# Small projections on 32-column strips, shared reciprocals, keys and values by transposes, and a gather in two halves, in a two-layer diffusion backbone

## The chip, the cores and the metric

The kernel runs on one core of one Trainium2 chip. The metric is the device time of one launch in microseconds (us), the median of several runs. Engines are named PE (TensorE; its weight loads are PEld), DVE (VectorE), ACT (ScalarE), POOL (GpSimd) and SP (SyncE, which issues the weight DMAs).

## The reference, cut to what matters

Two trunk layers work on 384 tokens (128 context, 256 latent) of width 1024, in fp32:

```
h = rms_norm(x, norm1_g) * (1 + sc1) + sh1            # sc, sh, g: silu(c) @ ada_w
proj = h @ w_in
A: q, k, v = silu(short_conv(proj[qa, ka, va]))       # 12 channels of 128, 5 taps
   q = l2_norm(q) * 128**-0.5;  k = l2_norm(k)        # 4 heads each
   beta = sigmoid(...);  g = -rate * softplus(...)    # 16 small columns of proj
   chunked gated delta scan, forward and backward
B: chunkwise mLSTM scan over qb, kb, vb               # and 16 small gate columns
C: windowed grouped-query attention over qc, kc, vc, rotary on the latents
mixed = sig(ga) * (ya @ wa) + sig(gb) * (yb @ wb) + sig(gc) * (yc @ wc)
x += g1 * (mixed @ w_out)
h = rms_norm(x, norm2_g) * (1 + sc2) + sh2
aff = softmax(h @ w_router);  gates, idx = top_k(aff.T, cap)     # 16 experts
xs = h[idx]                                            # 32 latent + 16 context rows each
ye = (silu(xs @ w_gate) * (xs @ w_up)) @ w_down * gates
x += g2 * scatter_add(ye, idx)
```

## The kernel before

The hidden state stands as hT, eight tiles of 128 features by 384 tokens. One Fori over the two layers holds everything. Each engine has its own program, written out in order by hand; what an engine produces is counted on a semaphore (a mark in a "track" such as conv_act or ring_used), and the consumer waits for that count. All weights come as 2 MB blocks (eight tiles of 128x512) that SP loads in order into a ring of four slots, six for the experts; per layer 32 blocks and then 48 of the experts (gate, up, down for each of 16). A slot is loaded again when PE has marked the block in it as used.

PE uses three forms of projection. `channels` (L757) has the weights stationary and 384 tokens moving, eight matmuls for 128 output features. `tokens` (L764) has 128 tokens of hT stationary and 256 or 512 weight columns moving, for output in token layout. `ada_block` (L805) puts 32 matmuls of 128 columns side by side on four strips of 32 partitions. Transposes are all at L729.

The stages of a layer, in PE's order, with the lines that matter here:

- norm and modulation; then the small projection of the 32 gate columns (L825: 24 matmuls with hT stationary, 32 columns moving).
- twelve conv channels (L757). Behind each, ACT copies the bank to a padded tile (copies are all at L1514), DVE does five taps (L1922, L1924), ACT does silu. For the eight q and k heads ACT squares (L1602), PE sums the squares over the 128 partitions with a matrix of ones (L845), ACT takes the root (L1611), and DVE a reciprocal (L1931) and a multiply (L1933), each on 128x384. The gates' chain (DVE, ACT, and prefix sums on PE, L853 and L856) stands ahead of the fourth channel.
- delta rule: decay rows (L874), k-k products (L880), token-layout transposes, four ada blocks (L805), then the inverses and the scan.
- mLSTM: queries and keys by channels, transposes of the delta rule's output, the keys once more in token layout (L764, 128x256), a selection product (L1076), q-k product (L1089), values (L764, 128x512).
- attention: q and k by channels, k and v in token layout (L764, 128x256), rotary (L1244).
- merge of the branches, output projection, second norm.
- router: L1382 (24 matmuls, 16 columns moving), softmax and top-k on DVE, the selection matrices sel (L2308) and, weighted, selG (L2310), transposes of selG, and the gather (L1429, L1431), in which hidden rows in token layout are stationary and sel moves; DVE copies out (L2317, L2318), and POOL copies one expert's columns to a tile of its own (L717) and clears a tile (L710).
- experts, a Fori of two turns of eight: gate and up (L1460), silu, product on DVE (L2336), transposes, down (L1485), copies, and a combine (L1443, L2327) that scatters four experts at a time back to xT.

```
def squared_length(j):
    pe.wait_ge(done["conv_act"], at("conv_act", l, ("sq", j)))
    ...
    mm(PS[:, 4 + j % 4, 0:N], ones, sq_in[:, j % 2, :], start=True, stop=True)...
```

## Time and profile before

| | us |
|---|---|
| median of 3 runs | 2071.69 (2068.59 to 2072.93) |
| profiled execution, its own time | 2070.92 |
| its span | 2069.2 |
| PE busy | 1771.0 (86%) |
| DVE busy | 666.7 (32%) |
| ACT busy | 496.2 (24%) |
| POOL busy | 154.3 (7%) |
| moved by DMA | 344.63 MB, 167 GB/s over the span |

Times in the trace count from the span's start. Most fp32 matmuls leave two records, so x16 in a row of the timeline is eight matmuls; transposes leave one. A row of the timeline is a run of alike instructions: its start, its length, engine, line, shapes, count, and in brackets the idle time of the engine ahead of it with what ended it. Layer 0 runs to about 1022 us, layer 1 behind it with the same stages.

### The profile page before, as it was taken

Reading aid. Unit: us, or ns where it says so; the run is one execution under the profiler, and the core shown is the slowest. Engines: PE = TensorE matmul, PEld = TensorE weight load, DVE = VectorE, ACT = ScalarE, POOL = GpSimd, SP = SyncE. Lnnn points to the kernel's source line nnn. Section 1 sums busy time; section 2 is a strip of 40 time slices with the busy share of each in tenths; the row PEclk is TensorE's granted clock in tenths of the full one; section 3 lists DMA queues with packets and bytes.
Section 4 is the critical chain, followed back from the end, with each engine's and each line's share of the span. In section 5 each row is a group of like instructions: output and inputs, shape, how many; then the busy total and the mean of one; then the engine's idle time right before and its main releaser. Section 6 shows DMA issues by size and latency. Waiting matters only on the chain.

```text
span 2069.2 us, 30757 instructions
## 1 busy us (share of the span) xinstructions
PE 1771.0 (86%) x12119; PEld 1039.6 (50%) x12119; DVE 666.7 (32%) x1306; ACT 496.2 (24%) x1124; POOL 154.3 (7%) x186
## 2 busy tenths in 40 slices
PE   4888998999899778888669799899998995888884
PEld 3557865556555442232255587546565554323222
DVE  1395433221421241222217843414033114212124
ACT  3372441021500201111045515212033003011111
POOL 2004110100000000000100221101000000000000
PEclk9799999999999879999869999999999996999997
DMA  9324411505112409999942324123431143499990
GB/s 333 117 82 165 166 57 41 87 22 167 53 69 110 174 0 368 393 394 394 324 175 82 135 102 145 47 82 46 145 85 41 41 162 122 158 394 394 395 364 31
DMA packets 165633, 344.63 MB, mean 167 GB/s; under 512 B 21130, under 2 KB 23266, under 8 KB 165376
## 3 DMA queue, kind: packets, MB, share of 16 engines
q1 hardware_dynamic: 162560, 338.44, 45.9%
q0 software_dynamic: 2944, 4.39, 1.0%
q8 instruction: 92, 1.51, 0.3%
q14 instruction: 37, 0.30, 0.0%
HBM read 339.39 MB, written 3.41 MB: 166 GB/s over the span
## 4 chain that ended last, share of the span: by engine, by line
PE 71%; DMA 9%; DVE 7%; issue 4%; ACT 4%; DVEq 2%; PEld 1%; ACTq 0%; POOL 0%; SPq 0%; PEldq 0%; POOLq 0%
PE PS L757 19%; DMA arena<-in_w_expert_up_dram 9%; PE PS L1460 8%; PE PS L764 6%; PE PS L1368 4%; PE PS L1327 4%; PE PS L1485 3%; PE PS L729 3%; PE PS L1257 3%; PE PS L1193 2%; PE PS L919 1%; PE PS L805 1%; PE PS L1429 1%; PE PS L911 1%; ACT hT L1550 1%
## 5 line engine op out<-in xcount | busy, mean ns | idle before, releaser
L757 PE MATMUL PS<-hT,ring 128*128 128x384 f32 x1312 | 443.6, 494 | 5.1 <-issue 3.0
L757 PEld LDWEIGHTS PS<-hT,ring 128*128 128x128 f32 x1312 | 250.4, 192 | 183.2 <-issue 20.2
L1460 PE MATMUL PS<-ring,arena 128*48 128x512 f32 x768 | 232.4, 607 | 29.5 <-DMA arena<-in_w_expert_up_dram 16.4
L1514 ACT ACTIVATE arena<-PS 128x512 f32<-128x512 f32 (+3 forms) x246 | 114.1, 497 | 465.3 <-PE PS L729 146.2
L1460 PEld LDWEIGHTS PS<-ring,arena 128*48 128x48 f32 x768 | 69.2, 125 | 186.7 <-issue 163.1
L764 PE MATMUL PS<-ring,hT 128*128 128x256 f32 (+1 forms) x384 | 132.2, 502 | 11.6 <-DVE arena L2105 11.1
L729 PE MATMUL PS<-const,arena 128*128 128x128 f32 (+2 forms) x389 | 55.3, 284 | 71.6 <-DVE arena L2336 35.0
L1460 PE MATMUL PS<-arena 128*48 128x512 f32 x256 | 116.2, 608 | 0.0
L764 PEld LDWEIGHTS PS<-ring,hT 128*128 128x128 f32 x384 | 74.5, 197 | 62.4 <-issue 44.0
L2336 DVE TENSOR_TENSOR arena<-arena,PS 48x512 f32<-48x512 f32 x32 | 22.1, 690 | 237.8 <-ACT arena L1795 237.8
L729 PEld LDWEIGHTS PS<-const,arena 128*128 128x128 f32 (+2 forms) x389 | 44.6, 154 | 104.1 <-issue 68.8
L1795 ACT ACTIVATE arena<-PS 48x512 f32<-48x512 f32 x32 | 18.9, 589 | 301.5 <-PE PS L1460 301.5
L1368 PE MATMUL PS<-arena,ring 128*128 128x384 f32 x256 | 85.0, 487 | 2.7 <-DVE arena L2241 2.7
L1327 PE MATMUL PS<-arena,ring 128*128 128x384 f32 x256 | 85.7, 487 | 1.5 <-ACT arena L1514 1.5
L1257 PE MATMUL PS<-hT,ring 128*128 128x384 f32 x256 | 85.5, 488 | 0.0
L1485 PE MATMUL PS<-arena 128*48 128x512 f32 x256 | 64.8, 652 | 5.1 <-ACT arena L1514 5.1
L1368 PEld LDWEIGHTS PS<-arena,ring 128*128 128x128 f32 x256 | 48.5, 190 | 37.3 <-issue 3.9
L1327 PEld LDWEIGHTS PS<-arena,ring 128*128 128x128 f32 x256 | 48.5, 190 | 36.7 <-issue 3.3
L1485 PE MATMUL PS<-ring,arena 128*48 128x512 f32 x256 | 61.4, 623 | 5.3 <-ACT arena L1514 5.3
L2239 DVE TENSOR_TENSOR arena<-PS,arena 128x384 f32<-128x384 f32 x32 | 17.9, 558 | 147.8 <-PE PS L1327 147.8
L2342 DVE COPY arena<-PS 32x512 f32<-32x512 f32 x32 | 22.0, 688 | 133.5 <-PE PS L1485 133.5
L1257 PEld LDWEIGHTS PS<-hT,ring 128*128 128x128 f32 x256 | 47.7, 190 | 31.9 <-issue 1.3
(326 smaller groups left out, 2262.7 us busy)
## 6 DMA issues: line engine op xcount, KB each, us to landing
ring<-in_w_expert_gate_dram SPq DMA_DIRECT2D x32, 2048.0 KB, 16.0
ring<-in_w_in_dram SPq DMA_DIRECT2D x26, 2048.0 KB, 9.7
ring<-in_ada_w_dram SPq DMA_DIRECT2D x24, 2048.0 KB, 16.8
ring<-in_w_expert_up_dram SPq DMA_DIRECT2D x16, 2048.0 KB, 19.4
ring<-in_w_expert_down_dram SPq DMA_DIRECT2D x16, 2048.0 KB, 18.8
arena<-in_w_expert_up_dram SPq DMA_DIRECT2D x16, 2048.0 KB, 21.6
arena<-in_w_expert_down_dram SPq DMA_DIRECT2D x16, 2048.0 KB, 19.0
ring<-in_w_out_dram SPq DMA_DIRECT2D x4, 2048.0 KB, 7.8
```

The lines of the kernel that those rows point to most:

```text
L729: return nc.tensor.transpose(out, in_, ident[0:n, 0:n])
L757: ins = mm(out, w[:, k, 128 * c:128 * c + 128], hT[:, k, :], start=k == 0, stop=k == KT - 1)
L764: ins = mm(out, hT[:, k, 128 * t:128 * t + 128], w[:, k, c0:c1], start=k == 0, stop=k == KT - 1)
L1193: ins = mm(PS[:, product_bank(c), 0:N], w[:, k, 128 * c:128 * c + 128], yT[0][:, k, :], start=k == 0, stop=k == 3)
L1257: ins = mm(PS[:, 7 - c % 2, 0:N], w[:, k, 128 * (c % 4):128 * (c % 4) + 128], hT[:, k, :], start=k == 0, stop=k == KT - 1)
L1327: ins = mm(PS[:, 2 + n % 2, 0:N], w[:, k, 128 * c:128 * c + 128], yT[r][:, k, :], start=k == 0, stop=k == 3)
L1368: ins = mm(PS[:, 4 + c % 4, 0:N], w[:, k, 128 * (c % 4):128 * (c % 4) + 128], mixT[:, k, :], start=k == 0, stop=k == KT - 1)
L1460: ins = mm(PS[64 * n:64 * n + ROWS, u % 2, :], xs_e[:, u % 2, k, :], expert_view(3 * u + n)[:, k, :], start=k == 0, stop=k == KT - 1)
L1485: ins = mm(PS[64 * n:64 * n + ROWS, 4 + u % 2, :], hidT[:, u % 2, f, :], expert_view(3 * u + 2, 4)[:, f, 512 * n:512 * n + 512], start=f = ...
L1514: return f(out, in_, ACT.Copy)
L2336: TT(hid[0:ROWS, u % 2, :], silu_g[64:64 + ROWS], PS[64:64 + ROWS, u % 2, :], ALU.mult)\
L2342: V.tensor_copy(ye_s[o:o + CAP_S, u // PACK, 512:1024], PS[64:64 + CAP_S, 4 + u % 2, :])
```

## The change

The edits, in the order of the stages:

- The gates' columns and the router's (padded from 16 to 32) become stationary, 128x32, and all 384 tokens move. The eight partial products of the contraction go to four strips of 32 partitions, two to each (`partial_sums`); DVE copies the strips to rstd, and three matmuls with rstd stationary and a 0/1 matrix add the strips up and turn the result to tokens (`folded`).
- The squared lengths of four channels go to four strips of one bank, 32 equal rows each. ACT takes one root and DVE one reciprocal for four channels. Eight new matmuls (`length_of`) spread a strip's first row over 128 partitions, and DVE multiplies from there.
- The gates' chain is laid between the channels: its DVE, ACT and PE pieces stand behind channels 0 to 6, and PE waits for its end after channel 7.
- The k-k products of all three tiles stand before the token-layout transposes, and the decay rows after the last multiply.
- The mLSTM keys in token layout come from six transposes of the keys that are there by channels; ACT copies them. The selection product moves between the last two key channels. DVE's products with z move behind the mLSTM exponents' arguments.
- The attention values come by channels, and are turned by four transposes, one of them for the context's keys.
- Only experts 0 to 7 are gathered (for latents) ahead of the expert loop, experts 8 to 15 inside experts 2 to 5 (`gather_later`); selG and its transposes are made four experts at a time inside the loop (`weights_turned`). POOL's copies and clearing are gone; the experts read the gathered tile itself. The loop is written out for all 16, and the combine is spread over the next four experts, two tiles of xT each.

```
+def partial_sums(w, bank):
+    for k in range(KT):
+        q = k % 4
+        ins = mm(PS[32 * q:32 * q + 32, bank, 0:N], w[:, k, :], hT[:, k, :], start=k < 4, stop=k >= 4)
+    return ins
+def folded(bank, n):
+    for t in range(TILES):
+        ins = mm(PS[:, bank, N + n * t:N + n * t + n], rstd[:, 128 * t:128 * t + 128], K("fold")[:, 0:n],
+                 start=True, stop=True)
+    return ins
-for t in range(TILES):
-    for k in range(KT):
-        ins = mm(PS[:, 4, 32 * t:32 * t + 32], hT[:, k, 128 * t:128 * t + 128], w_small[:, k, :],
-                 start=k == 0, stop=k == KT - 1)
+partial_sums(w_small, 4).then_inc(T["gate_pe"].mark("part"), 1)
...
+LENGTHS_AFTER = {7: (0, 1, 2), 8: (3,), 10: (4, 5, 6, 7)}
+def squared_length(i):
+    pe.wait_ge(done["conv_act"], at("conv_act", l, ("sq", i)))
+    q = i % 4
+    mm(PS[32 * q:32 * q + 32, 5 - i // 4, 0:N], ones[:, 0:32], sq_in[:, i % 2, :], ...)
+def length_of(i):
+    if i % 4 == 0:
+        pe.wait_ge(done["conv_dve"], at("conv_dve", l, ("inv", i // 4)))
+    if i == 3:
+        pe.wait_ge(done["conv_dve"], at("conv_dve", l, ("unit", 0)))
+    if i == 4:
+        pe.wait_ge(done["conv_dve"], at("conv_dve", l, ("unit", 3)))
+    own = slice(32 * (i % 4), 32 * (i % 4) + 32)
+    mm(PS[:, LENGTH_BANK[i], 0:N], K("lead")[own, :], nrm[own, i // 4, :], start=True, stop=True)...
+for j in range(12):
     blk = conv_channels(blk, j)
+    if j == 0:
+        pe.wait_ge(done["gate_dve"], at("gate_dve", l, "part"))
+        folded(4, 32).then_inc(T["gate_pe"].mark("proj"), 1)
     if j == 4:
+        prefix_sums()
+    if 2 <= j < 10:
+        squared_length(j - 2)
+    if j == 7:
         pe.wait_ge(done["gate_dve"], at("gate_dve", l, "done"))
-    if j >= 4:
-        squared_length(j - 4)
+    for i in LENGTHS_AFTER.get(j, ()):
+        length_of(i)
...
 # DVE, behind the taps of channel j
-if j >= 4:
-    i = j - 4
-    v.wait_ge(done["conv_act"], at("conv_act", l, ("root", i)))
-    V.reciprocal(nrm[:, i % 2, 0:N], nrm[:, i % 2, 0:N])
-    v.drain()
-    TT(qkvT[:, i, :], qkvT[:, i, :], nrm[:, i % 2, 0:N], ALU.mult)...
+if j in (5, 9):
+    n = j // 5 - (j == 5)
+    v.wait_ge(done["conv_act"], at("conv_act", l, ("root", n)))
+    V.reciprocal(nrm[:, n, 0:N], nrm[:, n, 0:N]).then_inc(T["conv_dve"].mark(("inv", n)), 1)
+for i in LENGTHS_AFTER.get(j, ()):
+    v.wait_ge(done["conv_pe"], at("conv_pe", l, ("bc", i)))
+    TT(qkvT[:, i, :], qkvT[:, i, :], PS[:, LENGTH_BANK[i], 0:N], ALU.mult)...
...
-for k in range(KT):   # experts, gather
-    for t in (1, 2):
-        mm(PS[:, 2 + k % 2, :], h_tok[:, t, 128 * k:128 * k + 128], sel[:, t].rearrange("p e s -> p (e s)"), ...)
+for k in range(KT):
+    for t in (1, 2):
+        mm(PS[:, 2 + k % 4, 0:256], h_tok[:, t, 128 * k:128 * k + 128],
+           sel[:, t, 0:HALF, :].rearrange("p e s -> p (e s)"), start=t == 1, stop=t == 2)
...
+def gather_later(u):
+    n = 2 * LATER.index(u)                      # LATER = (2, 3, 4, 5)
+    for k in (n, n + 1):
+        for t in (1, 2):
+            ins = mm(PS[:, 2 + (u + 1) % 2, 256 * (k - n):256 * (k - n) + 256], h_tok[:, t, 128 * k:128 * k + 128],
+                     sel[:, t, HALF:NE, :].rearrange("p e s -> p (e s)"), start=t == 1, stop=t == 2)
+def weights_turned(u):                          # u % 4 == 3
+    pe.wait_ge(done["ex_dve"], at("ex_dve", l, (u - 1, "sel")))
+    ...
+    for t in range(TILES):
+        ins = tr(PS[:, 6, 128 * t:128 * t + 128], selG[:, t].rearrange("p e s -> p (e s)"))
```

PE's order at three places, as the built programs have it. First the start of a layer, from the gates' projection to the prefix sums (small holds the gates' weights; K("fold") lies in const). Before:

```order
L825 MATMUL PS<-small,hT 128x32 [waits nrm_act]
L825 MATMUL PS<-small,hT 128x32 x23
L739 REGISTER_ALU
L757 MATMUL PS<-hT,ring 128x384 [waits slot_in0]
L757 MATMUL PS<-hT,ring 128x384 x23
L850 ISA
L853 MATMUL PS<-small,const 128x8 [waits gate_dve]
```

The same place after:

```order
L806 MATMUL PS<-hT,small 32x384 [waits nrm_act]
L806 MATMUL PS<-hT,small 32x384 x7
L719 REGISTER_ALU
L737 MATMUL PS<-hT,ring 128x384 [waits slot_in0]
L737 MATMUL PS<-hT,ring 128x384 x7
L864 ISA
L812 MATMUL PS<-const,rstd 128x32 [waits gate_dve]
L812 MATMUL PS<-const,rstd 128x32 x2
L737 MATMUL PS<-hT,ring 128x384 x16
L832 ISA
L834 MATMUL PS<-arena,const 32x384 [waits conv_act]
```

Eight wide matmuls stand where 24 narrow ones stood, the fold waits for DVE behind the first channel, the prefix sums have moved on behind the fifth channel, and the first squared length stands behind the third.

Second, PE ahead of the mLSTM values, before (L1076 is the selection, L1089 the q-k product):

```order
L764 MATMUL PS<-ring,hT 128x256 [waits mp_act]
L764 MATMUL PS<-ring,hT 128x256 x7
L1071 REGISTER_ALU
L1076 MATMUL PS<-small,const 128x3x4 [waits ml_dve]
L1076 MATMUL PS<-small,const 128x3x4 x3
L764 MATMUL PS<-ring,hT 128x256 x8
L764 MATMUL PS<-ring,hT 128x256 [waits mp_dve]
L764 MATMUL PS<-ring,hT 128x256 x7
L1082 REGISTER_ALU
L1089 MATMUL PS<-arena 64x64 [waits mp_act]
L1089 MATMUL PS<-arena 64x64 x23
L1150 REGISTER_ALU [waits slot_in1]
```

After, from behind the transposes of the delta rule's output:

```order
L1086 ISA
L709 MATMUL PS<-const,arena 128x128 [waits mp_act]
L709 MATMUL PS<-const,arena 128x128 x5
L1098 MATMUL PS<-arena 64x64 x24
L1159 REGISTER_ALU [waits slot_in1]
L744 MATMUL PS<-ring,hT 128x512 [waits mp_act]
L744 MATMUL PS<-ring,hT 128x512 x15
```

Six transposes replace the 24 matmuls, the wait for DVE (mp_dve) in their midst is gone, and the values wait for ACT's copies (mp_act) behind the q-k product.

Third, PE from the counts of the router to the first expert, before (the first L729 rows turn selG):

```order
L729 MATMUL PS<-const,arena 128x128 [waits rt_act,rt_dve]
L729 MATMUL PS<-const,arena 128x128 x5
L1420 REGISTER_ALU
L729 MATMUL PS<-const,arena 128x128 [waits rt_dve]
L729 MATMUL PS<-const,arena 128x128 x2
L1420 REGISTER_ALU
L729 MATMUL PS<-const,arena 128x128 [waits rt_dve]
L729 MATMUL PS<-const,arena 128x128 x2
L1429 MATMUL PS<-arena 128x512 x2
L1431 MATMUL PS<-arena 128x256
```

The same place after:

```order
L1421 MATMUL PS<-arena,const 128x48
L1423 REGISTER_ALU
L1429 MATMUL PS<-arena 128x256 [waits rt_act,rt_dve]
L1429 MATMUL PS<-arena 128x256
L1431 MATMUL PS<-arena 128x256
```

The twelve transposes are gone from here, and the gather's matmuls for the latents have 256 columns instead of 512.

## Rows read from the trace of the kernel before

**Rows 1.** The page, chain that ended last, share of the span by engine.

```profile
PE 71%; DMA 9%; DVE 7%; issue 4%; ACT 4%; DVEq 2%; PEld 1%; ACTq 0%; POOL 0%; SPq 0%; PEldq 0%; POOLq 0%
```

**Rows 2.** Timeline of PE at the start of layer 0.

```profile
54.45 10.45 PE L825 MATMUL PS<-small,hT 128*128 128x32 f32 x48 [7.83 <-ACT hT L1550]
64.70 17.96 PE L757 MATMUL PS<-hT,ring 128*128 128x384 f32 x48
82.50 1.40 PE L853 MATMUL PS<-small,const 128*128 128x8 f32 x12
...
98.69 0.91 PE L845 MATMUL PS<-arena,const 128*128 128x384 f32 x2 [3.19 <-ACT arena L1602]
99.44 7.02 PE L757 MATMUL PS<-hT,ring 128*128 128x384 f32 x16
...
119.06 5.32 PE L757 MATMUL PS<-hT,ring 128*128 128x384 f32 x16
124.22 0.81 PE L845 MATMUL PS<-arena,const 128*128 128x384 f32 x2
...
142.88 2.74 PE L874 MATMUL PS<-arena,const 128*128 128x512 f32 x6
152.12 1.97 PE L880 MATMUL PS<-arena 128*64 128x128 f32 x16 [6.50 <-DVE arena L1933]
...
162.48 1.93 PE L805 MATMUL PS<-ring,condT 128*2 128x128 f32 x64 [1.25 <-ACT arena L1514]
```

**Rows 3.** Timeline of DVE in the conv stage of layer 0.

```profile
117.64 2.54 DVE L1931 RECIPROCAL arena<-arena 128x384 f32<-128x384 f32 x1
...
121.23 2.71 DVE L1924 SCALAR_TENSOR_TENSOR arena<-arena,vecT 128x388 f32<-128x388 f32 x4
```

**Rows 4.** Timeline of PE, mLSTM keys and values of layer 0.

```profile
317.83 3.62 PE L764 MATMUL PS<-ring,hT 128*128 128x256 f32 x16
321.29 0.96 PE L1076 MATMUL PS<-small,const 128*128 128x12 f32 x8
...
331.36 5.73 PE L764 MATMUL PS<-ring,hT 128*128 128x256 f32 x16 [5.57 <-DVE arena L2105]
337.44 0.93 PE L1089 MATMUL PS<-arena 64*64 64x64 f32 x48 [0.35 <-issue]
338.30 14.00 PE L764 MATMUL PS<-ring,hT 128*128 128x512 f32 x32
```

**Rows 5.** Timeline of PE, attention keys and values of layer 0.

```profile
489.81 10.52 PE L764 MATMUL PS<-ring,hT 128*128 128x256 f32 x48
```

**Rows 6.** Timeline of PE, router to first expert of layer 0.

```profile
717.99 10.42 PE L1382 MATMUL PS<-small,hT 128*128 128x16 f32 x48 [12.47 <-ACT hT L1550]
728.25 1.95 PE L729 MATMUL PS<-const,hT 128*128 128x128 f32 x8
...
748.84 3.40 PE L1429 MATMUL PS<-arena 128*128 128x512 f32 x4
...
770.09 7.08 PE L1460 MATMUL PS<-ring,arena 128*48 128x512 f32 x32 [2.38 <-POOL arena L717]
```

**Rows 7.** Windows: length, busy us (instructions) by engine, PE clock, DMA share, GB/s.

```profile
800.00:810.00 10.00, 7.82 (x40) 2.47 (x38) 0.69 (x1) 0.92 (x2) 0.51 (x1) 1.00 1.04 395
1010.00:1020.00 10.00, 7.60 (x39) 3.84 (x38) 4.94 (x13) 1.17 (x2) 0.00 (x0) 1.00 1.05 387
```

**Rows 8.** Windows of 2 us in the conv stage, columns as in rows 7.

```profile
58.00:60.00 2.00, 2.00 (x11) 2.00 (x11) 0.00 (x0) 0.00 (x0) 0.00 (x0) 0.50 1.07 391
100.00:102.00 2.00, 2.00 (x4) 1.01 (x3) 1.85 (x4) 1.36 (x4) 0.00 (x0) 0.50 0.00 0
```

**Rows 9.** Timeline of DVE, top-k and selection of layer 0.

```profile
735.21 1.76 DVE L2283 COPY arena<-arena 48x128 f32<-48x128 f32 x1
...
742.17 1.90 DVE L2308 TENSOR_TENSOR arena<-const,small 128x512 f32<-128x512 f32 x3
```

**Rows 10.** Timeline of POOL in the same stretch.

```profile
735.09 1.81 POOL L710 MEMSET hT<- 128x2048 f32 x1 [239.30 <-PE PS L729]
```

More of the change, by code:

```diff
@@ L838, in conv_channels @@
                     return blk + (j % 4 == 3)
-                def squared_length(j):
-                    pe.wait_ge(done["conv_act"], at("conv_act", l, ("sq", j)))
-                    if j >= 4:
-                        pe.wait_ge(done["conv_act"], at("conv_act", l, ("root", j - 4)))
-                    mm(PS[:, 4 + j % 4, 0:N], ones, sq_in[:, j % 2, :], start=True, stop=True).then_inc(T["conv_pe"].mark(("ss", j)), 1)
-                for j in range(3):
-                    blk = conv_channels(blk, j)
@@ L857, in _ @@
[L857 to L861 removed]
+                def squared_length(i):
+                    pe.wait_ge(done["conv_act"], at("conv_act", l, ("sq", i)))
+                    q = i % 4
+                    mm(PS[32 * q:32 * q + 32, 5 - i // 4, 0:N], ones[:, 0:32], sq_in[:, i % 2, :], start=True, stop=True)\
+                        .then_inc(T["conv_pe"].mark(("ss", i)), 1)
+                def length_of(i):
[6 more added lines that the diff above has]
+                    own = slice(32 * (i % 4), 32 * (i % 4) + 32)
+                    pe.sem_inc(apart["pe"], 1)
+                    mm(PS[:, LENGTH_BANK[i], 0:N], K("lead")[own, :], nrm[own, i // 4, :], start=True, stop=True)\
+                        .then_inc(T["conv_pe"].mark(("bc", i)), 1)
@@ new lines, in prefix_sums @@
+                def prefix_sums():
+                    pe.wait_ge(done["gate_dve"], at("gate_dve", l, "lf"))
+                    for t in range(TILES):
+                        for d in range(2):
+                            mm(PS[:, 6, 16 * t + 8 * d:16 * t + 8 * d + 8], K(f"tri{d}"), g_lf[:, t, d, :], start=True, stop=True)
+                    gl = g_lf.rearrange("p t d h -> p (t d h)")
+                    for n, m in enumerate(("block", "half0", "half1")):
+                        ins = mm(PS[:, 6, 48 + 48 * n:96 + 48 * n], K(m), gl, start=True, stop=True)
+                    ins.then_inc(T["gate_pe"].mark("cum"), 1)
@@ L1379, in _ @@
                 pe.wait_ge(done["nrm_act"], at("nrm_act", l, "h1"))
-                for t in range(TILES):
-                    for k in range(KT):
-                        ins = mm(PS[:, 7, 16 * t:16 * t + 16], hT[:, k, 128 * t:128 * t + 128], w_rt[:, k, :],
-                                 start=k == 0, stop=k == KT - 1)
-                ins.then_inc(T["rt_pe"].mark("logit"), 1)
+                partial_sums(w_rt, 7).then_inc(T["rt_pe"].mark("part"), 1)
                 def hidden_turned(t):
@@ L1496, in _ @@
+                for k in range(KT):
+                    combine(NE // PACK - 1, k)
             pe.wait_ge(final_dve, 1)
@@ new lines, in gates_done @@
+                def gates_done():
+                    v.wait_ge(done["gate_act"], at("gate_act", l, "ecum"))
+                    TT(kbg_f, beta.rearrange("p t (d h) -> p t d h", d=2), e_cum, ALU.mult)\
+                        .then_inc(T["gate_dve"].mark("done"), 1)
+                    for n, (g, where_, p, first) in enumerate(SCAN):
+                        for d, (t, c) in enumerate(where_):
+                            half = slice(CH * c, CH * c + CH)
+                            V.tensor_copy(e_step[half, n, :], e_cum[half, t, d, :])
@@ L2349, in _ @@
+                for k in range(KT):
+                    combine(NE // PACK - 1, k)
                 v.drain()
```

563 lines of the change are left out of this document (275 added, 288 removed).

## Prediction, made before the changed kernel was run

> **What bounds the kernel now.** First view: the chain that ended last, by engine [rows 1]. TensorE holds 71% of it, DMA 9%, VectorE 7%. So the kernel is a sequence of stages on TensorE, with one stretch (the experts) that hangs on the weight stream, and a few places where TensorE stands still for another engine. What a change is worth has to be read from its stage, and I read four stages, each in layer 0; layer 1 repeats them some 1012 us later, so each gain counts twice.
>
> Second view: TensorE's timeline at the start of a layer [rows 2]. The gates' projection (L825) runs from 54.45 to 64.70, three channels follow, then prefix sums, then the other channels with a squared length behind each. One channel takes 5.16 us (119.06 to 124.22), so one 384-column matmul 0.645. The reader is to see three things: L825 does 24 matmuls of 32 columns in 10.45 us, 0.435 each, two thirds of the price of a 384-column one; TensorE stops 3.19 us at 98.69 for ScalarE; and 6.50 us before L880 at 152.12 for L1933, VectorE's last multiply. VectorE's timeline says why [rows 3]: one reciprocal begins at 117.64 and takes 2.54, then 1.05 goes to a multiply and the first tap, and the four taps that close the period end at 121.23 + 2.71 = 123.94: 6.3 us per channel against TensorE's 5.16 + 0.645 = 5.8. VectorE is the slower one and the difference is paid at 152.12.
>
> Third view: TensorE between the mLSTM queries and its values [rows 4]: the keys' token layout costs 24 matmuls of 256 columns, with a stop of 5.57 for VectorE (L2105) in the middle. The same 24-matmul pattern for attention takes 10.52 [rows 5]. Fourth: from router to first expert [rows 6]: 717.99 to 770.09, 52.1 us, and then the experts with DMA full [rows 7].
>
> **The change, part by part, for one layer.**
>
> *A. Start of the layer: gates on strips, shared reciprocals, the gates' chain between channels.* TensorE's new sum, from 54.45:
> - Partial sums, eight 384-column matmuls on four 32-column strips. Nothing of this shape is in the trace. The nearest is L805 [rows 2]: 64 records, which are 32 matmuls of 128 columns to four strips, in 1.93 us, 0.060 each, where 128 columns alone would be 0.215 (a third of 0.645). So strips run 3.6 side by side, and 8 x 384 columns cost 24 x 0.060 = 1.45. Not side by side they cost 8 x 0.645 = 5.2.
> - Twelve channels 61.9. Fold: three matmuls at half L825's price (the clock was 0.50 there [rows 8]), 0.65. Prefix sums: the 82.50 row's 1.40 and three more of their like, 2.1. Eight squared lengths 5.2.
> - Eight broadcasts of the reciprocals, new: 0.645 each, 5.2. Between 0 (32-row strips overlapping like L805's would leave 1.5) and 5.2 I take 5.2, since they are handed out one to three at a time.
> - The low clock at the start: the three channels from 64.70 took 17.96 against 15.5, so 2.5 stays.
> - Waits: 1.2, an estimate for the second reciprocal: it begins only after the tenth convolution (2.54 long), and the last four broadcasts stand right behind the eleventh channel.
>
> Sum 80.2, so the channels end near 134.6. VectorE does two reciprocals instead of eight: 12 x (6.3 - 2.54) + 2 x 2.54 = 50, and some 5 of gate work (an estimate): 55, well under 80, so it no longer sets the pace. Rows (L874) follow with 2.74 to 137.3. What stands before between the first L880 and L805 is 162.48 - 152.12 = 10.36; all of it remains, in another order, and the last convolution's silu is there before it is asked for (the last channel's end 134.6, taps 3.2, and about 1.1 for ScalarE's copy ahead of them and silu behind, 138.9; the three kk blocks keep TensorE busy beyond that). So L805 begins near 147.7 instead of 162.48: 14.8. I take **14.5**. Bounds: 17 with the broadcasts side by side; 5 if TensorE stops twice as it did at 98.69, where 3.19 of idle time also put the clock to 0.50 [rows 8] and made the next channel 7.02 instead of 5.32: 4.9 a stop.
>
> The gates' chain costs nothing as long as the channels cover it: fold after channel 0, logarithms after 1, sums after 4, exponentials after 6, and TensorE asks for its end only after channel 7, at least 5 us behind each hand-over. Uncovered, it would be the 3.19 stop again.
>
> Here a rule speaks against the strips. In [rows 4] TensorE goes from the 256-column matmuls to 64-row tiles (L1089) after 0.35 of issue time and back to whole-array matmuls with no gap (337.44 + 0.93 against 338.30). The Trainium skill, TensorEngine Tiling (Array Packing), section Key Properties, says that changing the tiling mode drains TensorE; it gives no price. By the rule there would be some 24 changes in the new channel stage (in and out of eight squared lengths, of three groups of broadcasts, of the partial sums); by the row one way costs at most 0.35 and the other nothing.
>
> *B. mLSTM keys by transposes.* Before, from 317.83 to the values at 338.30: 20.5 us, of which 5.57 is the wait for the bank that VectorE empties late. After, in that stretch: the selection (L1076) 0.8 (321.29, with what it overlaps), six 128-column transposes 0.7 (L729 at 728.25 has eight in 1.95 at half clock [rows 6], so 0.12 at full), the product (L1089) 0.87, and a wait for ScalarE's two copies of the keys: where TensorE waits for such a copy at 162.48 it is 1.25, the product covers 0.87 of it, and I take 0.5 for what is left. 20.5 - 2.9 = 17.6; **17.5**, bounds 15 (both copies and their hand-over exposed) and 18. VectorE's products with z are moved behind the exponents' arguments; they leave the keys' path with L2105.
>
> *C. Attention values by channels.* 24 matmuls, 10.52 [rows 5], become one channel 5.16, a wait for ScalarE's copy as at 162.48 (1.25), and four transposes 0.5: **3.6**. Bounds 2.5 and 4.5.
>
> *D. Router and gather.* Before: L1382 from 717.99, turned hidden rows (L729) at 728.25, 1.95 long [rows 6]. L1382's matmuls take 0.434 like L825's, so the clock is at half here too. After, at half clock: partial sums 2.9, the hidden rows 1.95 (VectorE's copy of the sums beneath them), fold 3 x 0.434 = 1.3; logits at 724.1, **4.1** sooner. Not side by side the partial sums cost 10.3: -3.3 instead. Top-k then stays as long, except for the copy L2283: 1.76 for 48x128 [rows 9], beside POOL's memset of 1.81 on the same microseconds [rows 10], which is gone; I put it at 0.25: **1.5**. So where selection began at 742.17 it begins at 736.6. Before: three products in 1.90 [rows 9], then the weighted ones and twelve transposes, gather at 748.84. After: two halves and one whole, 1.27, then gather at 737.9. Gather is 24 matmuls of 256 columns, 0.438 each [rows 5], 10.5, and 2.5 more for the low clock at its start, as much as the channels lose in A, so it ends near 750.9 and the first expert follows without POOL's copy (2.38 at 770.09). 770.09 - 750.9 = **19.2**. Bounds: 12 (strips one after another) and 21.5 (clock up at once).
>
> What the experts do with it: DMA share 1.04 from 800 to 1020 [rows 7], about 392 GB/s, 42 blocks of 2 MB to come after the first release, 5.35 us each. The stream starts when the first expert frees its blocks, so its end moves by the whole 19.2. Work added inside: the second half's gather, four times 1.75, and four times 0.4 of turned weights, about 8.6. TensorE is busy 7.82 of 10 there, so 220 us hold some 45 of idle time to hide it; if that cover were gone it would cost 8.6. The tail behind the last expert gets 0.5 longer, since turned weights now stand before it: D is **18.7**.
>
> **Sum.** 14.5 + 17.5 + 3.6 + 18.7 = 54.3, twice 108.6. The profiled execution took 2070.9 (its span 2069.2 and 1.7 around it), 0.8 under the median of the runs; 2070.9 - 108.6 gives **1962**.
>
> **Rivals.**
> 1. Strips run one after another. For it: no 32-column strip with 384 columns in the trace; against it: 0.060 at L805. Price 3.7 in A and 7.4 in D, 22 in all: 1984.
> 2. Every change of tiling costs issue time, 24 x 0.35 = 8.4 in A, 17 in all: 1979. This is where the skill's rule on draining leads. Against it: the way back without a gap.
> 3. Two stops per layer in the channel stage, at the two reciprocals, each 4.9 with the clock's fall: 20 in all, 1982.
> 4. The experts' stretch becomes bound by TensorE around experts 2 to 5, all 8.6 exposed: 17 in all, 1979. Against it: 45 us idle.
> 5. The other side: the clock. The new channel stage has 15 places per layer where TensorE waits for VectorE or ScalarE besides the pads (eight squares, two reciprocals, two multiplies, three of the gates). Where such a wait was long enough (98.69), it cost 4.9. All the gain is 54.3 per layer, so 11 of the 15 would have to stop it like that; from there on the kernel is slower, with all 15 by 2 x (73.5 - 54.3) = 38: 2109. Against it: the square at 124.22 shows no such stop.
>
> **How the numbers follow.** The forecast has 0.66, its own range 1950 (upper bounds: 17 + 18 + 4.5 + 21.5 less 0.5, twice 60.5) to 1972 (one stop more in A than counted). Rivals 1 to 4: 0.10, 0.06, 0.08, 0.05, all between 1979 and 1984; rival 5 0.05, most of it slower. Two of them together end beyond 1990. The range 1945 to 1988 leaves out rival 5, pairs, and the far end of the gains. About 0.2% (4 us) is what a measurement of this kernel can tell from no change: faster 0.94, same 0.02, slower 0.04.
>
> **What would show it.** Right: L805's successor near 147.7 instead of 162.48 with no wait for VectorE's multiply before the kk blocks; the partial sums near 1.5 and 2.9; values' matmuls about 3 us behind the last query/key channel; first expert near 20 us sooner after the router's start, and the DMA share still above 1.0 through the experts. Wrong: partial sums of 5 or 10; idle TensorE before a broadcast with the clock's windows at 0.50 behind it; DMA share below 1.0 in experts 2 to 5.

## The result, and the profile after

The changed kernel takes 1963.12 us (median of 4 runs, 1960.57 to 1965.23) against 2072.31 (4 runs, 2068.59 to 2074.13): a ratio of 0.9474, 95% interval 0.946 to 0.9488, 109 us less. The forecast was 1962, its own range 1950 to 1972. The profiled execution has a span of 1961.7, 107.5 under the one before.

The chain that ended last, by engine, answers to [rows 1]:

```profile
PE 71%; DMA 12%; DVE 6%; issue 4%; ACT 4%; DVEq 1%; PEld 1%; ACTq 0%; SPq 0%; PEldq 0%; POOL 0%; POOLq 0%
```

TensorE's share is what it was, of a shorter span. DMA's share rose from 9% to 12%: in each layer the chain now runs through five transfers of an expert's up block, of some 22 us each, where it ran through four before. The mean granted clock rose from 0.938 to 0.959; by these means (an estimate) half clock took some 128 us from the span before and 80 after, part of it in idle time, where it costs nothing. The gain has to be looked for by stage. First PE's timeline at the start of layer 0, which answers to [rows 2] (L806 partial sums, L812 fold, L737 channels, L834 squared lengths, L847 broadcasts, L882 rows, L888 kk, L785 ada blocks):

```profile
55.17 2.79 PE L806 MATMUL PS<-hT,small 128*32 128x384 f32 x16 [7.83 <-ACT hT L1561]
57.88 5.43 PE L737 MATMUL PS<-hT,ring 128*128 128x384 f32 x16
63.15 0.75 PE L812 MATMUL PS<-const,rstd 128*128 128x32 f32 x6
...
95.60 5.43 PE L737 MATMUL PS<-hT,ring 128*128 128x384 f32 x16
100.96 0.83 PE L834 MATMUL PS<-arena,const 128*32 128x384 f32 x2
...
108.18 0.92 PE L847 MATMUL PS<-arena,const 32*128 32x384 f32 x6
...
128.04 1.33 PE L847 MATMUL PS<-arena,const 32*128 32x384 f32 x8 [0.51 <-DVE arena L1961]
...
135.16 2.84 PE L882 MATMUL PS<-arena,const 128*128 128x512 f32 x6 [0.43 <-issue]
137.93 2.84 PE L888 MATMUL PS<-arena 128*64 128x128 f32 x48
...
147.58 1.93 PE L785 MATMUL PS<-ring,condT 128*2 128x128 f32 x64 [1.25 <-ACT arena L1525]
```

The stage runs from 55.17 to 147.58, 92.41 us, before 108.03. Eight partial sums took 2.71, the first channel right behind them 5.27, and the idle 6.50 before the k-k products is gone: what is left ahead of them is a stop of 0.51 for VectorE's second reciprocal and 0.43 of issue. Behind them TensorE waits three times for ScalarE's copies (1.18, 1.18 and 1.25; before, 0.15 and 1.25), and yet the stretch from the k-k products to the ada blocks is not longer, 9.65 for 10.36. A squared length takes 0.76 to the start of the channel behind it, and that channel 5.36 (95.60 to 100.96). Broadcasts are cheaper than one by one: to the channel behind them three take 0.85, four 1.26, and one by itself 0.84.

Windows of the same stretch (length, busy us by engine, PE clock, DMA share, GB/s) answer to [rows 8]; in this execution the clock is up at the first channel:

```profile
56.00:58.00 2.00, 2.00 (x17) 0.32 (x7) 0.00 (x0) 0.00 (x0) 0.00 (x0) 0.54 1.05 385
58.00:60.00 2.00, 2.00 (x7) 1.20 (x8) 0.56 (x1) 0.00 (x0) 0.00 (x0) 1.00 1.06 390
```

PE between the last key channel and the values, for [rows 4] (L709 transposes, L1098 q-k product, L744 values):

```profile
302.01 2.18 PE L709 MATMUL PS<-const,arena 128*128 128x128 f32 x18 [0.24 <-issue]
304.12 0.93 PE L1098 MATMUL PS<-arena 64*64 64x64 f32 x48
305.15 14.00 PE L744 MATMUL PS<-ring,hT 128*128 128x512 f32 x32
```

Eighteen transposes, twelve for the delta rule's output and six for the keys, take 2.11, and the values start 3.14 behind their beginning; before it was 21.8. PE at the attention's keys and values, for [rows 5]; key and value channels are one row of 32 records:

```profile
451.32 10.58 PE L737 MATMUL PS<-hT,ring 128*128 128x384 f32 x32 [1.06 <-ACT arena L1525]
462.48 0.77 PE L709 MATMUL PS<-const,arena 128*128 128x128 f32 x5 [0.58 <-ACT arena L1525]
463.09 2.32 PE L1252 MATMUL PS<-arena,const 128*128 128x256 f32 x10
```

ScalarE's copy is waited for 0.58, not 1.25. PE from the router to the first expert, for [rows 6]:

```profile
680.24 2.79 PE L806 MATMUL PS<-hT,small 128*32 128x384 f32 x16 [12.47 <-ACT hT L1561]
682.96 1.97 PE L709 MATMUL PS<-const,hT 128*128 128x128 f32 x8
684.73 1.30 PE L812 MATMUL PS<-const,rstd 128*128 128x16 f32 x6
...
698.63 2.08 PE L1429 MATMUL PS<-arena 128*128 128x256 f32 x4 [3.07 <-DVE arena L2347]
...
711.31 7.08 PE L1477 MATMUL PS<-ring,arena 128*48 128x512 f32 x32
```

31.07 us instead of 52.10. The experts' windows, for [rows 7], and PE at the last two experts, first after, then before:

```profile
750.00:760.00 10.00, 10.00 (x48) 2.85 (x44) 2.38 (x4) 1.17 (x2) 0.00 (x0) 1.00 1.04 392
940.00:950.00 10.00, 8.70 (x33) 2.32 (x33) 0.32 (x1) 0.10 (x1) 0.00 (x0) 0.83 1.04 396
```

```profile
925.46 7.07 PE L1477 MATMUL PS<-ring,arena 128*48 128x512 f32 x32 [2.60 <-DMA ring<-in_w_expert_up_dram]
...
941.30 0.63 PE L1477 MATMUL PS<-ring,arena 128*48 128x512 f32 x1 [2.42 <-DMA arena<-in_w_expert_up_dram]
...
950.00 0.49 PE L1443 MATMUL PS<-arena,hT 128*128 128x128 f32 x2
...
953.12 3.21 PE L1500 MATMUL PS<-arena 128*48 128x512 f32 x14
```

```profile
984.20 8.65 PE L1460 MATMUL PS<-ring,arena 128*48 128x512 f32 x32 [2.62 <-DMA ring<-in_w_expert_up_dram]
...
1000.07 0.63 PE L1460 MATMUL PS<-ring,arena 128*48 128x512 f32 x1 [0.86 <-DMA arena<-in_w_expert_up_dram]
```

The stream is full as before. The last expert waits 2.42 for its weights, and its matmuls then run partly at half clock (0.83 over the 10 us): 8.70 for gate and up against 7.0. In the kernel before the same befell the last expert but one, behind a wait of 2.62 (8.65); the last one then waited only 0.86 and ran at full clock. Half clock in the middle of the loop is made up by a shorter wait behind it; at the last expert nothing makes up for it. By stage, from the timelines of both layers (us; minus is longer than before; "keys" counts the moved selection product's 0.81 as its own):

```
stage                              layer 0: before  after   gain    layer 1: before  after   gain   forecast
gates' projection to ada blocks             108.03  92.41   15.6             106.56  92.49   14.1   14.5
ada blocks to delta's transposes            154.04 153.62    0.4             153.45 156.80   -3.4    0
keys: transposes to values                   21.78   3.95   17.8              21.75   3.95   17.8   17.5
attention: key channel to rotary             16.28  11.77    4.5              16.29  11.77    4.5    3.6
router to first expert                       52.10  31.07   21.0              52.08  31.16   20.9   19.2
first to last expert's down                 239.78 241.81   -2.0             239.61 242.28   -2.7   -0.5
```

Sum 57.3 and 51.3, together 108.6; the start of layer 0, the change of layers and the tail are 1.1 longer together.

### The profile page after: what moved, and what is told of

It reads as the page before. It is cut to its first block, busy times and chain, and to the rows that moved or that the text cites. A ratio compares the mean times of both kernels' runs of the same rounds, so it can differ in the third digit from the quotient of the medians.

```text
span 1961.7 us, 30102 instructions
## 1 busy us (share of the span) xinstructions
PE 1702.7 (87%) x11971; PEld 970.4 (49%) x11971; DVE 642.7 (33%) x1309; ACT 462.5 (24%) x1096; POOL 133.3 (7%) x152
## 4 chain that ended last, share of the span: by engine, by line
PE 71%; DMA 12%; DVE 6%; issue 4%; ACT 4%; DVEq 1%; PEld 1%; ACTq 0%; SPq 0%; PEldq 0%; POOL 0%; POOLq 0%
PE PS L737 22%; DMA arena<-in_w_expert_up_dram 11%; PE PS L1477 8%; PE PS L744 4%; PE PS L1377 4%; PE PS L1336 4%; PE PS L709 3%; PE PS L1265 3%; PE PS L1500 2%; PE PS L1202 2%; PE PS L919 2%; PE PS L927 1%; ACT hT L1561 1%; PE PS L931 1%; PE PS L785 1%
## 5 line engine op out<-in xcount | busy, mean ns | idle before, releaser
L737 PE MATMUL PS<-hT,ring 128*128 128x384 f32 x1344 | 449.8, 489 | 4.4 <-issue 2.3
L737 PEld LDWEIGHTS PS<-hT,ring 128*128 128x128 f32 x1344 | 251.9, 190 | 190.4 <-issue 18.9
L1525 ACT ACTIVATE arena<-PS 128x512 f32<-128x512 f32 (+5 forms) x252 | 116.5, 497 | 519.8 <-PE PS L1500 147.1
L2373 DVE TENSOR_TENSOR hT<-arena,PS 48x512 f32<-48x512 f32 x32 | 22.1, 690 | 248.9 <-ACT arena L1815 248.9
L744 PE MATMUL PS<-ring,hT 128*128 128x512 f32 x192 | 85.1, 597 | 0.7 <-issue 0.5
L1265 PE MATMUL PS<-hT,ring 128*128 128x384 f32 x256 | 85.5, 488 | 0.0
L2276 DVE TENSOR_TENSOR arena<-PS,arena 128x384 f32<-128x384 f32 x32 | 17.8, 558 | 148.5 <-PE PS L1336 148.5
L1954 DVE SCALAR_TENSOR_TENSOR arena<-arena,vecT 128x388 f32<-128x388 f32 x96 | 62.2, 648 | 7.2
L709 PE MATMUL PS<-const,arena 128*128 128x128 f32 (+2 forms) x281 | 40.0, 288 | 28.0 <-DMA arena<-in_final_norm_g_dram 14.9
L709 PE MATMUL PS<-const,hT 48*128 48x48 f32 (+1 forms) x200 | 29.2, 290 | 37.7 <-DVE hT L2373 28.2
L744 PEld LDWEIGHTS PS<-ring,hT 128*128 128x128 f32 x192 | 35.6, 190 | 44.6 <-issue 44.0
## 6 DMA issues: line engine op xcount, KB each, us to landing
ring<-in_w_expert_down_dram SPq DMA_DIRECT2D x16, 2048.0 KB, 19.2
```

The source lines that it names most:

```text
L709: return nc.tensor.transpose(out, in_, ident[0:n, 0:n])
L737: ins = mm(out, w[:, k, 128 * c:128 * c + 128], hT[:, k, :], start=k == 0, stop=k == KT - 1)
L744: ins = mm(out, hT[:, k, 128 * t:128 * t + 128], w[:, k, c0:c1], start=k == 0, stop=k == KT - 1)
L1265: ins = mm(PS[:, 7 - c % 2, 0:N], w[:, k, 128 * (c % 4):128 * (c % 4) + 128], hT[:, k, :], start=k == 0, stop=k == KT - 1)
L1525: return f(out, in_, ACT.Copy)
L1954: ins = STT(o, x, vecT[:, n:n + 1], o, ALU.mult, ALU.add)
```

## Experiments

All edit the changed kernel. Times are medians of 4 runs; the changed kernel's 1963.1 is the mark, and 3 us is about what such medians scatter. Stage times come from one profiled execution each; 1.5 to 3.4 us of loss to half clock come and go in stretches that an edit does not touch, so a stage that differs by so much shows nothing by itself.

**Strips given up.** Both projections as 24 narrow matmuls again, written straight to where the fold wrote:

```
-partial_sums(w_small, 4).then_inc(T["gate_pe"].mark("part"), 1)
+for t in range(TILES):
+    for k in range(KT):
+        ins = mm(PS[:, 4, N + 32 * t:N + 32 * t + 32], hT[:, k, 128 * t:128 * t + 128], w_small[:, k, :], ...)
+# the same for w_rt; both folds and DVE's two copies to rstd gone
```

> The changed kernel with the gates' and the router's projections as 24 narrow matmuls each again (no partial sums, no fold); the rest stays. Theory (the strips' time is on the path at both places): at the layer's start 10.45 us instead of 2.71 and a fold of 0.58, so 7.1 more, up to 9.5 if the first channels run at half clock again (2.5); at the router 10.26 instead of 2.72 + 1.30 around the hidden rows, some 4.4 more after the hidden rows got faster too. Together 23 to 28 us over two layers: 1986 to 1991. Rival (VectorE still paces the channel stage and hides the start): only the router shows, 9 us: 1972.

1989.28, ratio 0.9607 (0.9589 to 0.9625): 26 more, inside the theory's 23 to 28. PE at the start of layer 0:

```profile
54.42 10.45 PE L819 MATMUL PS<-small,hT 128*128 128x32 f32 x48 [7.83 <-ACT hT L1564]
64.68 17.74 PE L737 MATMUL PS<-hT,ring 128*128 128x384 f32 x48
```

10.26 us, and the three channels behind it 17.74; the granted clock is 0.50 all the way to 68 us, in the narrow matmuls and in the first of the channels. By stage, the layer's start is 8.8 and 8.9 longer and the router 4.6 and 4.2. The rival falls.

**Side by side, or cheap by itself?** First the order of strips, 0 0 1 1 2 2 3 3:

```
-q = k % 4
-ins = mm(PS[32 * q:32 * q + 32, bank, 0:N], w[:, k, :], hT[:, k, :], start=k < 4, stop=k >= 4)
+q = k // 2
+ins = mm(PS[32 * q:32 * q + 32, bank, 0:N], w[:, k, :], hT[:, k, :], start=k % 2 == 0, stop=k % 2 == 1)
```

> The eight partial products go to the strips in pairs, 0 0 1 1 2 2 3 3 instead of 0 1 2 3 0 1 2 3; same work, same sums. Theory (neighbours in the order run side by side only on different strips): two at a time at best, so a set takes 5.2 us at half clock (four of 1.29) instead of 2.7, at four places: 10 us more, 1973. Rival (a matmul of 32 stationary columns is cheap by itself, whatever stands next to it): the set stays at 2.7, and the time at 1963.

1961.86, ratio 0.9471 (0.9447 to 0.9496): no change, and the set takes 2.74:

```profile
54.49 2.81 PE L806 MATMUL PS<-hT,small 128*32 128x384 f32 x16 [7.83 <-ACT hT L1561]
57.23 5.67 PE L737 MATMUL PS<-hT,ring 128*128 128x384 f32 x16
```

My theory, that only neighbours overlap, fell; the rival would explain this too. So all eight on one strip (with the other three cleared on DVE, and start and stop at the ends):

```
+ins = mm(PS[0:32, bank, 0:N], w[:, k, :], hT[:, k, :], start=k == 0, stop=k == KT - 1)
```

> All eight partial products go to one strip (the other three are cleared ahead of the fold), at both projections. With two in a row on a strip the set took 2.74, as with neighbours on different strips, so either reading is still open. Theory (each strip works through its own list beside the others, two matmuls of 1.28 at half clock either way): eight in one list take some 10.3 us instead of 2.7 while the clock is at half; 5 to 7.5 more at each of four places, as far as the clock stays low: 20 to 30 in all, 1983 to 1993. Rival (a 32-column matmul costs about 0.34 at half clock, whatever its neighbours): 2.7 stays; 1963, or up to 1965 for the clearing.

1978.05, ratio 0.955 (0.9532 to 0.9569), 15 more:

```profile
54.82 8.28 PE L805 MATMUL PS<-hT,small 128*32 128x384 f32 x16 [7.83 <-ACT hT L1560]
63.03 5.43 PE L737 MATMUL PS<-hT,ring 128*128 128x384 f32 x16
```

The set takes 8.21 instead of 2.71 (7.86 at the router), not the 10.3 of half clock throughout, because the clock rises inside it (0.81 from 60 to 62). That is not a cheap matmul: strips do run side by side, and each works through its own list. By stage the four places cost 5.3 to 5.5 each, 21.7 together, as the theory had it. The total is 15 only; of the difference the experts' loops, which the edit does not touch, give back 3.7, because half clock did not fall on their last expert in this execution.

**Keys by matmuls at the new place,** copied by ScalarE:

```
-for t in (2, 0, 1):
-    for j in range(2):
-        ins = tr(PS[...], qkbT[:, 2 + j, 128 * t:128 * t + 128])
+for t in (2, 0, 1):
+    ins = tokens(blk, t, PS[:, 6 if t == 2 else 7, 256 * (t % 2):256 * (t % 2) + 256], 256, 512)
```

> The mLSTM keys in token layout by 24 matmuls of 256 columns again, but at the new place, into the new banks and copied by ScalarE, so that the old stop for VectorE does not come back. Theory (the gain of 17.6 a layer is the work, 10.5 less 0.7, and the stop with the low clock behind it, 7.8): 9.8 a layer more, 20 us: 1983. Rival (the stop was a matter of place, not of who copies, and returns behind the copies): another 5 to 8 a layer, 1993 to 1998.

1982.1, ratio 0.957 (0.9553 to 0.9587): 19 more, the theory's 20.

```profile
304.58 10.53 PE L744 MATMUL PS<-ring,hT 128*128 128x256 f32 x48
315.21 0.93 PE L1095 MATMUL PS<-arena 64*64 64x64 f32 x48
```

24 matmuls in 10.63 and no stop behind them. So of 17.8 a layer some 10 are work; the rest is the stop for VectorE's late copy and the half clock behind it [rows 4]. That part stays away with the matmuls back, so it came from the new place, the new banks and ScalarE's copies; which of the three, this run does not part.

**Attention's values by matmuls,** with VectorE's three copies as before:

```
-channels(blk, 1, PS[:, 5, 0:N]).then_inc(T["ap_pe"].mark("v"), 1)
+for t in range(TILES):
+    tokens(blk, t, PS[:, 5 + t, 0:256], 0, 256).then_inc(T["ap_pe"].mark(("kv", t)), 1)
```

> The attention's keys and values in token layout by 24 matmuls of 256 columns again, copied by VectorE as before. Theory (all of it is TensorE's time on the path): 4.5 us a layer, the stretch 16.3 again instead of 11.8; 9 us: 1972. Rival (VectorE's rotary chain or ScalarE's copies end the stretch anyway): under 2 us, 1963 to 1965.

1970.19, ratio 0.9507 (0.949 to 0.9524): 7 more. In layer 0 the stretch is 16.28 again, so the theory (9) stands, within the scatter.

**All experts gathered at once:**

```
+for n in range(4):                                  # ahead of the expert loop, banks 2 to 5
+    pe.wait_ge(done["rt_dve"], at("rt_dve", l, ("xs", 4 + n)))
+    ...                                             # the body of gather_later
-if u in LATER:
-    gather_later(u)
```

> Experts 8 to 15 are gathered ahead of the expert loop too: sixteen matmuls of 256 columns (0.43 each) move from experts 2 to 5 to the place before the first expert. Theory (the loop follows the weight stream, whose start hangs on the first expert): 6.9 us a layer more, 14 us: 1977, the loop's own length unchanged within 1. Rival (TensorE bounds the loop around experts 2 to 5): the loop gets shorter by what the start gets later, 1963 to 1966.

1977.36, ratio 0.9542 (0.952 to 0.9564): 14 more, as the theory said.

```profile
712.45 7.07 PE L1452 MATMUL PS<-arena 128*128 128x256 f32 x32
```

The added set takes 7.0, and from the first expert to the last one's down matmuls it is 242.2 us, with the later gather 241.8. So work taken out of the loop does not shorten it: the loop follows the stream, and rival 4 falls. In the changed kernel TensorE is busy 10.00 of 10 us from 750 to 760 and up to the seventh expert it hardly waits for weights (0.13); from the eighth on it waits for them ahead of every expert, 0.7 to 2.6 us, and that room hides the added work.

**Reciprocals of their own.** Whole-array squares behind channels 4 to 11, root, reciprocal and multiply per channel, no broadcasts:

```
-if j in (5, 9): ...                                 # DVE: one reciprocal for four
-for i in LENGTHS_AFTER.get(j, ()): ...              # DVE: multiply from the broadcast
+if j >= 4:
+    i = j - 4
+    v.wait_ge(done["conv_act"], at("conv_act", l, ("root", i)))
+    V.reciprocal(nrm[:, i % 2, 0:N], nrm[:, i % 2, 0:N])
+    v.drain()
+    TT(qkvT[:, i, :], qkvT[:, i, :], nrm[:, i % 2, 0:N], ALU.mult)...
```

> Squared length over the whole array, root, reciprocal and multiply for each q and k channel by itself again, from the fifth channel on; strips for the gates, the gates' chain between channels and the order behind them stay. Theory (VectorE, at 6.2 us a channel against TensorE's 5.8, falls behind once more, and the idle time before the k-k products comes back, less the eight broadcasts and the waits that go): a layer 2 to 4 us longer, 4 to 8 in all: 1967 to 1971. Rival (the shared reciprocals carry most of the gain at the layer's start): over 10 us, 1973 and more. Rival (the gates' chain between the channels alone frees VectorE): no change or up to 6 us faster, since the broadcasts are gone: 1957 to 1963.

1981.18, ratio 0.9559 (0.9539 to 0.958), 18 more. My theory (4 to 8) falls and the first rival (over 10) stands; but the edit had brought in a wait of 3.15 us for a bank. The same with the prefix sums in bank 7:

> Each q and k channel's own root, reciprocal and multiply as in the run before, with the prefix sums in another bank, so that the wait of 3.15 us for that bank, which the earlier edit brought in and the kernel before did not have, is gone. The decay rows stay behind the last multiply. Theory (VectorE's lag is the cost, 8.36 of idle time before the rows, less what the broadcasts took): some 6 to 7 a layer, 12 to 14 in all: 1975 to 1977. Rival (the extra wait made most of it): under 6 in all, 1969 or less.

1982.7, ratio 0.9577 (0.955 to 0.9603), 20 more, above the theory's 12 to 14: the wait did not go, it moved to the gates. PE in layer 0:

```profile
108.38 7.12 PE L735 MATMUL PS<-hT,ring 128*128 128x384 f32 x16 [2.62 <-DVE small L1935]
...
142.51 5.13 PE L880 MATMUL PS<-arena,const 128*128 128x512 f32 x6 [8.36 <-DVE arena L1963]
...
157.22 3.48 PE L783 MATMUL PS<-ring,condT 128*2 128x128 f32 x64 [1.25 <-ACT arena L1523]
```

VectorE behind on reciprocals finishes the gates' chain late (2.62 at 108.38, and the next channel takes 6.95 to the square behind it); at the end the rows wait 8.36 for its last multiply and run at half clock. So giving up the shared reciprocals alone costs some 10 of the 15 us gained at the layer's start. Part of that is the gates' chain, which lies between the channels without a stop only while VectorE is not behind.

**A visit to the strips.** Squares two and two, then squares and broadcasts in fours (four square buffers, all behind channels 5 and 9):

```
+if j in (3, 5, 7, 9):
+    squared_length(j - 3)
+    squared_length(j - 2)
```

> The squared lengths stand two and two, behind channels 3, 5, 7 and 9, instead of one behind each of channels 2 to 9. In the changed kernel a squared length with the channel behind it takes 6.12 us, on the whole array before it took 5.81. Theory (the 0.31 belongs to the change of tiling in and out): four such changes fewer a layer, 1.2 us, 2.5 in all: 1960.6; in the trace 0.3 less for every second channel. Rival (it belongs to each strip matmul): the sum of squares and channels stays within 0.3 a layer, 1963.

1957.0, ratio 0.945 (0.9425 to 0.9475). A pair takes 0.77 to the channel behind it, no more than one alone:

```profile
57.81 6.95 PE L737 MATMUL PS<-hT,ring 128*128 128x384 f32 x16
...
94.56 0.84 PE L834 MATMUL PS<-arena,const 128*32 128x384 f32 x4
95.33 10.59 PE L737 MATMUL PS<-hT,ring 128*128 128x384 f32 x32
```

A visit less saves its 0.76 and the 0.2 by which the channel behind it is longer: 0.95 a pair, four pairs, 3.8 a layer. In layer 1 the stage is 3.4 shorter, 89.13; in layer 0 only 1.0, since the first channel took 6.79 there (57.81 to 64.60, partly at half clock) where the changed kernel's took 5.27 with the same code. The 6 measured fit that better than the 2.5 that I had expected, but the two intervals still overlap.

```
+LENGTHS_AFTER = {7: (0, 1, 2, 3), 10: (4, 5, 6, 7)}
+LENGTH_BANK = (6, 7, 5, 4, 6, 7, 5, 4)
+sq_in = carve(arena, 0, 4, N)
+if j in (5, 9):
+    for i in range(4):
+        squared_length(j - 5 + i)
```

> The squared lengths stand in two groups of four, behind channels 5 and 9, and the broadcasts in two groups of four, behind channels 7 and 10; the same matmuls. In pairs the squares took 0.77 to 0.87 a pair against 2 x 0.76. Theory (each visit to strips costs about 0.6 and each matmul in it 0.1 to 0.2): two visits of about 1.0 for eight squares instead of 8 x 0.76, and two of 1.26 for the broadcasts instead of 2.95 in three: 4.5 a layer, 9 in all: 1954. Rival (four at once wait for ScalarE's squares or VectorE's multiplies come too late for the rows): a stop of 1 to 3 a layer, 1956 to 1960.

1950.82, ratio 0.9416 (0.9395 to 0.9437), under the changed kernel's interval: the best kernel here, 12 us faster than the change (9 expected; by stage 4.3 and 4.9).

```profile
92.66 0.85 PE L837 MATMUL PS<-arena,const 128*32 128x384 f32 x8
93.44 10.59 PE L737 MATMUL PS<-hT,ring 128*128 128x384 f32 x32
```

Four squares take 0.78 where one took 0.76. So the price is that of a visit, whose length is one 384-column matmul and a little; a strip used alone wastes the other three.

**The fold sooner,** behind half of the first tile's transposes, on top of that:

```
-hidden_turned(0)
+hidden_turned(0, (0,))
 pe.wait_ge(done["rt_dve"], at("rt_dve", l, "part"))
 folded(7, NE).then_inc(T["rt_pe"].mark("logit"), 1)
+hidden_turned(0, (1,))
```

> The same, and at the router the fold stands behind the first half of the first tile's transposes instead of behind all of them, so that the logits are there sooner. Theory: 0.9 a layer at half clock, 1.8 more than the run without: 1952. Rival (VectorE's copy is not ready by then, or the second half delays the transposes of the affinities by as much): the same as without.

1951.74, ratio 0.9418 (0.9397 to 0.9439): inconclusive. At its place it works, the affinities' transposes stand 7.34 behind the router's start instead of 8.20. But the five count matmuls behind them then took 2.37 at half clock in layer 0, where they had taken 1.31, and the gather began no sooner (18.67 behind the router's start, without the edit 18.39); and 1.7 us is below the scatter.

**A stop on purpose.** Prefix sums asked for two channels earlier:

```
-if j == 4:
+if j == 2:
     prefix_sums()
```

> The prefix sums are asked for behind channel 2 instead of channel 4, so that TensorE stands still until VectorE has the gates' logarithms: some 6 us (74.2 to 80.4 in layer 0). Theory of the dear stop (the clock falls behind it and the next channel takes 1.7 more): about 8 a layer, 16 in all: 1979, with windows at 0.50 behind the stop. Rival (a stop costs its own length): 12 us, 1975, no window below 1.00 but the stop's. Rival (later waits absorb it): under 8 us.

1981.56, ratio 0.9563 (0.9542 to 0.9583), 18 more. PE and windows in layer 0:

```profile
81.94 2.73 PE L854 MATMUL PS<-small,const 128*128 128x8 f32 x12 [6.23 <-DVE small L1919]
84.53 1.49 PE L857 MATMUL PS<-small,const 128*128 128x48 f32 x6
...
87.37 7.41 PE L737 MATMUL PS<-hT,ring 128*128 128x384 f32 x16
```

```profile
86.00:88.00 2.00, 2.00 (x4) 0.63 (x4) 0.00 (x0) 0.00 (x0) 0.00 (x0) 0.50 0.00 0
92.00:94.00 2.00, 2.00 (x8) 1.17 (x7) 0.00 (x0) 0.00 (x0) 0.00 (x0) 1.00 0.00 0
```

The stop is 6.23; behind it the clock is at 0.50, the two rows of prefix sums take 2.59 + 1.42 instead of 1.25 + 0.78, and the next channel 7.41 (5.43). With the squared length (1.42 for 0.76) that is about 4.6 of low clock on top of 6.2 of waiting. No later wait of the stage gave anything back: it is 12.3 longer in layer 0 and 10.6 in layer 1. The total is 18 and not 23 because stretches that the edit does not touch, the experts' loops among them, were shorter in this execution. Both rivals fall, and rival 5's price of 4.9 a stop was, if anything, low for a long one.

## Why the prediction was right

The four stages were the right ones, and each gained what it was given to within 2 us: keys 17.8 for 17.5, router 21.0 for 19.2, attention 4.5 for 3.6, start 15.6 and 14.1 for 14.5. Undoing the parts one by one cost 26, 19, 7, 14 and 18 to 20 us. They overlap (both the strips and the reciprocals touch the layer's start), so they need not add up to 109.

That the total fell within 1 us is partly luck; terms were mis-sized both ways, and where half clock fell differs between executions of the same code:
- *Partial sums and low clock.* Strips side by side was right: 1.45 at full clock predicted, 2.71 at half measured. But I added 2.5 for the first channels, as before; in this execution the clock rose at the first of them, and the start cost 2.8 instead of 3.95. That is chance in part: in the run with squares in pairs, the same code up to there, the first channel took 1.5 longer.
- *Broadcasts.* 5.2 was taken from the dear end; three visits took 2.95, nearer to the bound of 1.5 that I set aside.
- *Squared lengths.* 5.2 predicted, 6.1 measured, and the channel behind each 5.36 instead of 5.16. These eat what the broadcasts give back.
- *VectorE.* It no longer sets the pace, as said; its stop is 0.51 against 1.2 allowed. What I did not see is how much of A hangs on this: without it the gates' chain is uncovered too (2.62 in the second run with own reciprocals).
- *Attention.* ScalarE's copy was waited for 0.58, not 1.25: it is one copy of 384 columns, 0.49 long, where at the ada blocks two of 512 take 1.08. That is 0.7 of the 0.9 gained beyond the forecast.
- *Router.* The hidden rows' transposes stayed at half clock; to the fold they take 1.77, where I had taken the length of their row, 1.95. The low clock at the gather cost less: 12.7 for it all, 13.0 predicted. The rest of the 1.8 lies in top-k and selection: from the router's start to the gather 18.39, predicted 19.9. Of that, 1.0 is the five count matmuls, which ran at full clock (1.31 for 2.34). In layer 1 they took 2.37 at half clock again, and other pieces ran at full clock instead, so this gain too is chance in part.
- *Experts.* The end moved with the first release. The last up block is in place 230.0 us behind the first expert in both kernels (941.30 - 711.31; before, 1000.07 - 770.09). The loop is 2.0 longer all the same, where I had 0.5: 0.3 is the turned weights, 1.7 the half clock behind the last wait. The 1.7 depends on which expert it falls on: in the one-strip run, with the same loop, the last expert waited 0.70 and ran at full clock, and the loop took 240.3, 0.5 more than before.
- *Layer 1's delta rule* is 3.4 longer, in a stretch that the change does not touch. PE's row behind the gap ahead, and the windows of the changed kernel, show why:

```profile
1179.77 3.18 PE L947 MATMUL PS<-arena 64*128 64x64 f32 x37 [0.60 <-issue]
```

```profile
1178.00:1180.00 2.00, 1.40 (x26) 1.27 (x26) 0.35 (x1) 0.26 (x1) 0.83 (x1) 1.00 1.04 382
1182.00:1184.00 2.00, 2.00 (x34) 1.55 (x36) 1.01 (x2) 0.60 (x1) 0.97 (x1) 0.50 0.82 298
1184.00:1186.00 2.00, 2.00 (x44) 1.37 (x40) 1.93 (x2) 0.00 (x0) 2.00 (x3) 0.50 0.11 38
```

TensorE is busy, and the clock is at 0.50 all the same; the kernel before had 1.00 all through the same place of its program. What brought it down there, behind a gap of 0.60 us only, stays open. It is hardly the change: layer 0 has nothing of it, and of the twelve edited kernels, whose code there is the same, one alone shows it, the values by matmuls, in its layer 1.

Of the rivals, 1 (strips one after another) is out by the 8.21 of the one-strip run. Rival 2 put 24 changes of tiling at 0.35 each, 8.4 a layer. The rows show 0.2 more for the channel behind a strip (5.36 for 5.16) and 0.12 more for the squared length itself (0.76 for 0.645): 0.32 for going in and out, 2.5 for the eight visits, and so about 0.16 a change, under half of what I feared. The Trainium skill, TensorEngine Tiling (Array Packing), section Key Properties, says that changing the tiling mode drains TensorE; the trace agrees that a change costs time, but how much of the 0.32 is a drain no run shows. Rival 3 (two stops a layer at the reciprocals) did not come: one of 0.51, without a fall of the clock. Rival 5's mechanism is real, at 18 us for one long stop a layer, but the change brings no such stop.

## What to carry to other kernels

Price a stage by what ends its last wait: with eight reciprocals again instead of two, on an engine that was busy a third of the span, 10 of the 15 us gained at the layer's start are lost. Small projections belong on strips with the weights stationary, and strips are bought by the visit: fill all four before the next whole-array matmul. Ahead of a stretch that follows the weight stream, every microsecond before its first release counts once, and work inside it counts nothing as long as TensorE still waits for the stream behind it. And read a stage in more than one trace before explaining the last 2 us of it: half clock moved by as much between executions of the same code.

## What the runs showed of the hardware that was not expected

- Strips keep lists of their own: eight 384-column matmuls took 2.71 us at half clock with neighbours on different strips, 2.74 with two in a row on each, 8.21 all on one, the end of it at a clock that had risen. One squared length on a strip took 0.76 to the next channel, two 0.77, four 0.78 at full clock. The Trainium skill, TensorEngine Tiling (Array Packing), section Key Properties, says that different tiles execute in parallel; these runs agree, and show that the order of issue need not alternate.
- The length of a wait did not tell here what the clock did behind it. In the changed kernel's layer 0, waits for weights of 2.60, 2.43 and 2.40 us were followed by full clock, of 2.42, 2.29 and 2.27 by half clock; before, one of 2.45 by full and one of 2.62 by half clock. An expert at half clock took 1.7 longer, and the next wait was shorter by as much (0.71 behind the 2.29, 0.91 behind the 2.27). In layer 1 the clock fell behind a gap of 0.60 in work that had seemed dense.
